# Last feed-forward chunk in three token groups, and its down product tile by tile, in a two-layer streaming encoder

## The chip, the core and the metric

One core of a Trainium2 chip runs the whole program in one launch. The metric is device time in microseconds (us) of an execution; below it is the median of three runs. A profile of one more execution gives the span from its first to its last instruction and every instruction with its times. The engines are TensorE (PE; its weight loads are PEld), VectorE (DVE), ScalarE (ACT), GpSimd (POOL) and SyncE (SP), which only issues DMAs here.

## The reference

Two trunk layers of an encoder act on 1024 tokens of one new stream and 16 new tokens of each of 8 running streams, 1152 rows of width 1024. A layer is a mixer (attention and a linear recurrence, concatenated, one output projection) and a convolutional feed-forward part, each followed by a post-norm residual:

```python
def conv_ffn(x, conv_prev, w_up, conv_w, conv_b, w_down):      # D_FF = 2816, CONV_W = 3
    u = x @ w_up                                               # (T, 2 * D_FF)
    ue = jnp.concatenate([conv_prev, u], 1)                    # two rows before the stream's first
    c = conv_b
    for j in range(CONV_W):
        c = c + ue[:, j:j + T] * conv_w[j]                     # depthwise, causal
    a, b = jnp.split(c, 2, axis=-1)
    y = (jax.nn.silu(a) * b) @ w_down
    return y, ue[:, -(CONV_W - 1):]
...
x = layer_norm(DN_ALPHA * x + m, ...)
f, c = conv_ffn(x, ...)
x = layer_norm(DN_ALPHA * x + f, ...)
```

All of it is float32. The change touches only the end of `conv_ffn` and the layer norm behind it.

## The kernel before, in words

The change is in `phase_trunk`, which runs once per layer: mixer output projection, first norm, feed-forward, second norm. Each engine has its own instruction list written out by hand; the lists are ordered among themselves only by semaphores (`wait_ge`, `then_inc`). SyncE's list holds the DMAs.

**Numbers as pairs.** A float32 operand of a product is held as two rounded parts, hi and lo; ScalarE writes hi (a copy), GpSimd or VectorE writes lo (a subtraction), and `mm3` (lines 124 to 126) does three matmuls for one product.

**Feed-forward.** The 2816 channels go in NJ = 22 chunks of 128, for each of the halves a (`ab` = 0) and b (`ab` = 1). For chunk j, `up(j)` projects both halves for three groups of 384 tokens (`up_part(ab, q)`, 24 matmuls, result in PSUM bank q). ScalarE evicts each (`take`, into `u`), applies the convolution's centre tap for the whole half (`centre_tap`, into `cv`), VectorE adds the two other taps (`conv`), ScalarE does SiLU on half a, VectorE multiplies (`gate`), ScalarE writes hi of the result (`silu_and_hi`, into `gh`) and GpSimd lo (`split_gate`). GpSimd also puts the running streams' old rows into `u` (`halos`), keeps the last rows (`keep_state`) and splits the weights (`split_up`, `split_down`). `down(j)` is then the product with the chunk's rows of `w_down`, 9 token tiles by 2 halves of 512 columns, each added into `XM` (the residual, `x_or_mix` in the trace) by VectorE (`add`).

**Chunk order.** In the steady loop the order on TensorE is `up(j+1)`, `down(j)`. The last chunks differ: `up(LAST-1)` and `up(LAST)` run first (LAST = 21), and the down products of chunks 19, 20 and 21 are then accumulated in PSUM tile by tile. `tail_two(t)` does the 12 matmuls of chunks 19 and 20 for token tile t, `tail_end(t)` the 6 of chunk 21, in a pair of banks (`tail_pair`): tiles 0 to 3 take pairs 0 to 3, tile t from 4 on takes pair (t-4) mod 3. `tail_two` of tiles 0 to 3 comes first, then TensorE waits for the whole of chunk 21's gate (`gs`) and its down weights (`dsp`), and then runs `tail_end(0)` to `tail_end(3)` and, for each later tile, `tail_two(t)`, `tail_end(t)`.

**Second norm.** VectorE runs, per tile, `tail_add(t)` (PSUM into `XM`), `fnorm.stats(t)`, and `fnorm.rstd(t)`; between them ScalarE does a square root (`root`), and after them `normalise(t)`. GpSimd multiplies by the gain (`scale`), then GpSimd or, for the last tile (and for odd tiles in layer 1), VectorE adds the bias (`add_bias`). SyncE stores the tile.

**Transposes in layer 0 (`more`).** The next layer wants its input transposed, as a pair. TensorE transposes a finished tile with 8 matmuls into two banks (`f_t(t)`, banks `f_banks(t)`: 6 and 7, or 4 and 5 for t = 4, 6, 8), ScalarE writes hi (`f_hi(t)`, tile `xT_hi`), VectorE lo (`f_lo(t)`, tile `xT_lo`). In the order before, `f_t(t-3)` follows `tail_end(t)`, ScalarE's `f_hi(t-3)` precedes `root(t)`, and VectorE's `f_lo(t-3)` stands between `stats(t)` and `rstd(t)`, each for t from 3 to 8; the last three tiles follow behind. `f_t` waits for the bias of its tile and for the `f_lo` that frees its banks:

```python
            def f_t(t):
                pe.wait_ge(fnorm.xr, t + 1)
                if t == 0:
                    pe.wait_ge(ad, 1 + ADDED + 4)
                elif t == 4:
                    pe.wait_ge(ad, 1 + ADDED + 7)
                else:
                    pe.wait_ge(fxlo, t if t < 4 else t - 1)
```

`ad` counts adds: `1 + ADDED + n` is reached when n tiles of the tail are added.

Of the kernel before, what the change touches and what calls it, by code (L numbers as in the profile page):

```python
# [1738 lines left out]
def phase_trunk(c, block, layer, m, L):  # L1739
# [32 lines left out]

    ghz = m.at(tag + "gh_last", 16384, [P, TOK], R)
    glz = m.at(tag + "gl_last", 20992, [P, TOK], R)
    dhz = m.at(tag + "dhi_last", 25600, [P, D], R)
    dlz = m.at(tag + "dlo_last", 83200, [P, D], R)
    fg = m.at(tag + "ffn_gain", 87296, [P, D])
# [56 lines left out]
    if True:  # L1834
        @block.sync
        def _(sp):
# [263 lines left out]
        def _(act):  # L2100
# [104 lines left out]
            for t in range(NT):  # L2205
                if more and t >= 3:
                    f_hi(t - 3)
                fnorm.root(act, t)
                fnorm.normalise(act, t)
            if more:  # L2210
                for t in range(NT - 3, NT):
                    f_hi(t)

        @block.vector
        def _(dve):
# [90 lines left out]
            for t in range(NT):  # L2306
                tail_add(t)
                dve.wait_ge(ad, 1 + ADDED + t + 1)
                fnorm.stats(dve, flink, t)
# [4 lines left out]
                fnorm.rstd(dve, flink, t)
            if more:
                f_lo(NT - 3)
                f_lo(NT - 2)
            else:
# [235 lines left out]
```

## Time and profile before

| | |
|---|---|
| median of 3 runs | 3154.3 us |
| lowest, highest | 3151.47, 3155.53 us |
| the profiled execution | 3158.42 us |
| its span | 3156.7 us |
| its mean granted TensorE clock | 0.970 of full |
| PE busy | 2973.2 us, 94% |
| DVE busy | 1649.6 us, 52% |
| ACT busy | 1032.7 us, 33% |
| POOL busy | 839.4 us, 27% |

Busy time is that of instructions at work; waits, semaphores and the issue of DMAs are not in it. The span is shorter than the execution's time, which has a start and an end around it. Lines with L and a number are lines of the kernel printed above; a row of the timeline has the start in us from the span's start, the duration, the engine, the line, the operation, what it writes and reads, and in brackets how long the engine had been idle before it and what released it.

### The profile page before, as it was taken

To read this page: it belongs to the slowest core of one execution; us is meant where nothing else is said; L and a number is where in the kernel's file an instruction comes from. 1 tells how busy PE (TensorE), PEld (TensorE's weight loads), DVE (VectorE), ACT (ScalarE), POOL (GpSimd) and SP (SyncE) were. 2 spreads that over 40 slices of the span, in tenths; PEclk is the share of its full clock that TensorE was granted. 3 is DMA by queue.
4 is the path that set the end of the run, shared out by engine and by line. 5 is a ranking of instruction groups with operands and counts; after the bars stand their busy time and mean duration, and the time that the engine had idled before them with its cause. 6 is when DMAs were issued, how large, how long until landed. Compare 5 with 4: busy or idle time off the path is not lost. (4 is left out here: it accounts for less than half of the span.)

```text
span 3156.7 us, 42325 instructions
## 1 busy us (share of the span) xinstructions
PE 2973.2 (94%) x15759; PEld 2609.2 (83%) x15759; DVE 1649.6 (52%) x2579; ACT 1032.7 (33%) x2001; POOL 839.4 (27%) x700
## 2 busy tenths in 40 slices
PE   8899789998999999999997898998999999999996
PEld 6455457886889999999996897997889999999995
DVE  3466224566545555555555443345445555555555
ACT  4334212233342232223223353334342222322323
POOL 1245211111132233322336000011132223232325
PEclk9999899998999999999998997998999999999998
DMA  2100331113111111111111111113111111111111
GB/s 104 39 8 8 119 135 43 38 38 112 41 59 40 40 40 46 41 47 40 41 40 65 49 35 39 28 42 115 41 52 47 40 40 40 47 41 45 40 40 73
DMA packets 71879, 160.47 MB, mean 51 GB/s; under 512 B 19194, under 2 KB 33675, under 8 KB 70708
## 3 DMA queue, kind: packets, MB, share of 16 engines
q1 hardware_dynamic: 70612, 150.51, 15.1%
q0 software_dynamic: 1152, 8.39, 0.7%
q8 instruction: 76, 1.25, 0.2%
q14 instruction: 39, 0.32, 0.0%
HBM read 144.42 MB, written 15.11 MB: 51 GB/s over the span
## 5 line engine op out<-in xcount | busy, mean ns | idle before, releaser
L124 PE MATMUL psum<-xT_hi,tk_whi 128*128 128x384 f32 x2112 | 711.4, 337 | 2.9 <-POOL tk_wlo L1892 1.6
L125 PE MATMUL psum<-xT_lo,tk_whi 128*128 128x384 f32 x2112 | 710.2, 336 | 0.0
L126 PE MATMUL psum<-xT_hi,tk_wlo 128*128 128x384 f32 x2112 | 710.1, 336 | 0.0
L2272 DVE TENSOR_TENSOR x_or_mix<-x_or_mix,psum 128x512 f32<-128x512 f32 x684 | 466.0, 688 | 220.9 <-PE psum L126 220.6
L124 PEld LDWEIGHTS psum<-xT_hi,tk_whi 128*128 128x128 f32 x2112 | 397.6, 188 | 5.7 <-ACT tk_u L2128 4.2
L125 PEld LDWEIGHTS psum<-xT_lo,tk_whi 128*128 128x128 f32 x2112 | 397.6, 188 | 1.6
L126 PEld LDWEIGHTS psum<-xT_hi,tk_wlo 128*128 128x128 f32 x2112 | 397.4, 188 | 0.0
L2257 DVE SCALAR_TENSOR_TENSOR tk_c<-tk_u,tk_cw,tk_c 128x1168 f32<-128x1168 f32 x88 | 126.1, 1433 | 457.7 <-ACT tk_c L2136 457.7
L124 PE MATMUL psum<-tk_dhi,tk_gh 128*128 128x512 f32 x756 | 295.4, 391 | 4.6 <-DVE x_or_mix L2277 2.9
L126 PE MATMUL psum<-tk_dhi,tk_gl 128*128 128x512 f32 x756 | 295.2, 390 | 0.0
L125 PE MATMUL psum<-tk_dlo,tk_gh 128*128 128x512 f32 x756 | 295.2, 390 | 0.0
L1892 POOL TENSOR_TENSOR tk_wlo<-tk_wraw,tk_whi 128x1024 fp32r<-128x1024 f32 x88 | 230.9, 2624 | 184.8 <-ACT tk_whi L2115 184.8
L1916 POOL TENSOR_TENSOR tk_gl<-tk_g,tk_gh 128x1152 fp32r<-128x1152 f32 x42 | 112.4, 2677 | 511.8 <-ACT tk_gh L2143 511.8
L2259 DVE SCALAR_TENSOR_TENSOR tk_c<-tk_u,tk_cw,tk_c 128x1168 f32<-128x1168 f32 x88 | 219.3, 2492 | 11.1 <-DVE tk_c L2257 5.4
L2143 ACT ACTIVATE tk_gh<-tk_g 128x1152 fp32r<-128x1152 f32 x42 | 49.0, 1166 | 517.1 <-DVE tk_g L2267 517.1
L124 PEld LDWEIGHTS psum<-tk_dhi,tk_gh 128*128 128x128 f32 x756 | 142.2, 188 | 34.1 <-DVE x_or_mix L2277 3.3
L126 PEld LDWEIGHTS psum<-tk_dhi,tk_gl 128*128 128x128 f32 x756 | 142.0, 188 | 29.9
L125 PEld LDWEIGHTS psum<-tk_dlo,tk_gh 128*128 128x128 f32 x756 | 142.2, 188 | 28.6
L571 POOL TENSOR_SCALAR mla_p<-mla_p,mla_ri 128x128 f32<-128x128 f32 (+7 forms) x64 | 110.1, 1723 | 207.0 <-DVE mla_ri L600 207.0
L2125 ACT ACTIVATE tk_u<-psum 128x384 f32<-128x384 f32 x176 | 85.4, 487 | 235.7 <-PE psum L126 235.7
L2127 ACT ACTIVATE tk_u<-psum 128x256 f32<-128x256 f32 x88 | 33.8, 384 | 312.9 <-PE psum L126 312.9
L124 PE MATMUL psum<-tk_mix_w,xT_hi 128*128 128x512 f32 x288 | 121.1, 420 | 14.7 <-POOL tk_mix_w L813 8.1
(367 smaller groups left out, 5280.7 us busy)
## 6 DMA issues: line engine op xcount, KB each, us to landing
tk_wraw<-in_w_up SPq DMA_DIRECT2D x88, 512.0 KB, 3.6
tk_draw<-in_w_down SPq DMA_DIRECT2D x44, 512.0 KB, 3.6
x_or_mix<-in_c_ckvT SPq DMA_DIRECT2D x8, 1024.0 KB, 5.7
s_ckv<-in_c_ckv POOLq DMA_DIRECT2D x8, 1024.0 KB, 5.0
retw_raw<-in_w_ret SPq DMA_DIRECT2D x32, 256.0 KB, 3.8
tk_mix_wraw<-in_w_out SPq DMA_DIRECT2D x16, 512.0 KB, 3.6
glaw_raw<-in_w_gla SPq DMA_DIRECT2D x32, 192.0 KB, 3.5
x_or_mix<-in_xT SPq DMA_DIRECT2D x9, 512.0 KB, 9.9
```

The costliest lines, as they stand in the source:

```text
L124: nc.tensor.matmul(out, a[0], b[0], start=first, stop=False)
L125: nc.tensor.matmul(out, a[0], b[1], start=False, stop=False)
L126: return nc.tensor.matmul(out, a[1], b[0], start=False, stop=last)
L571: nc.gpsimd.tensor_scalar(p, p, ri[:, u % 4:u % 4 + 1], None, ALU.mult).then_inc(scl, 1)
L1892: nc.gpsimd.tensor_tensor(wlo[:, ab].rearrange("p k n -> p (k n)"), wraw[:, ab, :], whi[:, ab].rearrange("p k n -> p (k n)").bitcast(F), A ...
L1916: nc.gpsimd.tensor_tensor(lo, gf[:], hi.bitcast(F), ALU.subtract).then_inc(gs, 1)
L2125: last = nc.scalar.activation(u[:, ab, 2 + q * GRP:2 + (q + 1) * GRP], PS[:, q, 0:GRP], ACT.Copy)
L2127: nc.scalar.activation(u[:, ab, 2 + 2 * GRP:US], PS[:, 2, 0:SEQ - 2 * GRP], ACT.Copy)
L2143: nc.scalar.activation(hi, gf[:], ACT.Copy).then_inc(ghd, 1)
L2257: nc.vector.scalar_tensor_tensor(cv[:, ab, 2:], u[:, ab, 1:UW - 1], cw[:, ab, col4(j, 1)], cv[:, ab, 2:], ALU.mult, ALU.add).then_inc(cch, 1)
L2259: nc.vector.scalar_tensor_tensor(cv[:, ab, 2:], u[:, ab, 0:UW - 2], cw[:, ab, col4(j, 0)], cv[:, ab, 2:], ALU.mult, ALU.add).then_inc(cvd, 1)
L2272: nc.vector.tensor_tensor(x, x, PS[:, down_bank(n), :], ALU.add).then_inc(ad, 1)
```

## The change

What it does:

- `up(LAST)` runs its six parts in the order (a,0), (a,1), (b,0), (b,1), (a,2), (b,2) instead of a's three and then b's three. The banks stay the group's number, and the waits for evictions follow the new order.
- The centre tap, convolution, SiLU, gate, hi and lo of chunk 21 are done in three groups of 384 tokens (the third has the running streams' rows). `ghz` and `glz`, one tile each, become three tiles each (`gz`), and the places of the last down weights and of the norm's gain move.
- TensorE does `tail_two(0)`, `tail_two(1)`, then `tail_end(0)`, `tail_end(1)`, and from tile 2 on `tail_two(t)`, `tail_end(t)`; tiles 0, 3 and 6 wait for their group of the gate. The bank pair of tile t is t mod 3 throughout, so pairs 0 to 2 are used and banks 6 and 7 are free.
- In layer 0 a table `F_AFTER` says after which tile's `tail_end` which `f_t` comes; `f_hi` and `f_lo` follow one tile later. `f_t(0)` waits for no add any more.
- The norm's gain is loaded when the last up part is done, the bias when the third group's convolution is done.

```diff
-    tail_pair = lambda t: t if t < 4 else (t - 4) % 3
-    f_banks = lambda t: 4 if t >= 4 and t % 2 == 0 else 6
+    tail_pair = lambda t: t % 3
+    f_banks = lambda t: 0 if t in (4, 6, 8) else 6
+    F_AFTER = {4: (0,), 5: (1,), 6: (2,), 7: (3,), 8: (4, 5)}
+    CONVS = 2 * NJ + 4
+    GROUPS = ((0, GRP, GRP), (GRP, 2 * GRP, GRP), (2 * GRP, SEQ, UW - 2 - 2 * GRP))
...
@@ sync
-            sp.wait_ge(us, 2 * NJ)
+            sp.wait_ge(um, 6 * NJ)
             sp.dma_start(fg[:], A["ln_ffn_g"][layer].partition_broadcast(P)).then_inc(fgl, 16)
-            sp.wait_ge(cvd, 2 * NJ)
+            sp.wait_ge(cvd, CONVS)
...
@@ gpsimd
+            def split_gate_group(g):
+                pool.wait_ge(ghd, LAST + g + 1)
+                nc.gpsimd.tensor_tensor(gz[1][g][:], gf[:, g * GRP:(g + 1) * GRP], gz[0][g][:].bitcast(F), ALU.subtract).then_inc(gs, 1)
...
             halos(LAST)
+            split_gate_group(0)
+            split_down(LAST, None)
+            split_gate_group(1)
             for ab in range(2):
-                keep_state(LAST, ab, 6 * LAST + 3 * ab + 3)
-            split_down(LAST, None)
-            split_gate(LAST, None)
+                keep_state(LAST, ab, 6 * LAST + 5 + ab)
+            split_gate_group(2)
...
@@ tensor
             def f_t(t):
                 pe.wait_ge(fnorm.xr, t + 1)
-                if t == 0:
-                    pe.wait_ge(ad, 1 + ADDED + 4)
-                elif t == 4:
+                if t == 4:
                     pe.wait_ge(ad, 1 + ADDED + 7)
-                else:
+                elif t:
                     pe.wait_ge(fxlo, t if t < 4 else t - 1)
...
             def tail_two(t):
-                pe.wait_ge(ad, 1 + ADDED + (0 if t < 4 else TAIL_AFTER[t - 4] + 1))
+                pe.wait_ge(ad, 1 + ADDED + max(t - 2, 0))
...
             def tail_end(t):
-                tail_down(t, (ghz, glz), (dhz, dlz), False, True).then_inc(dm, 1)
+                if t % 3 == 0:
+                    pe.wait_ge(gs, LAST + t // 3 + 1)
+                for half in range(2):
...
-            up(LAST)
+            for p, (ab, q) in enumerate(ORDER0):
+                if q == 0:
+                    pe.wait_ge(us, 2 * LAST + ab + 1)
+                pe.wait_ge(ur, 6 * LAST + (-2, -1, 1, 2, 0, 5)[p])
+                up_part(ab, q)
             pe.wait_ge(gs, LAST - 1)
             pe.wait_ge(dsp, LAST - 1)
             pe.wait_ge(ur, 6 * NJ)
-            for t in range(4):
-                tail_two(t)
-            pe.wait_ge(gs, LAST + 1)
+            tail_two(0)
+            tail_two(1)
             pe.wait_ge(dsp, LAST + 1)
             for t in range(NT):
-                if t >= 4:
+                if t >= 2:
                     tail_two(t)
                 tail_end(t)
-                if more and t >= 3:
-                    f_t(t - 3)
+                if more:
+                    for f in F_AFTER.get(t, ()):
+                        f_t(f)
...
@@ scalar
             def hi_down(j, par):
                 act.wait_ge(ld, 16 * j + 16)
+                if par is None:
+                    act.wait_ge(um, 6 * LAST + 5)
...
-            for ab in range(2):
-                act.wait_ge(cvd, 2 * LAST + ab - 1)
-                act.wait_ge(sk, 2 * LAST + ab - 1)
-                for q in range(3):
-                    take(ab, q, 6 * LAST + 3 * ab + q)
-                centre_tap(LAST, ab, 6 * LAST + 3 * ab + 3)
-            hi_down(LAST, None)
-            silu_and_hi(LAST, None)
+            for p, (ab, q) in enumerate(ORDER0):
+                if q == 0:
+                    act.wait_ge(cvd, 2 * LAST + ab - 1)
+                    act.wait_ge(sk, 2 * LAST + ab - 1)
+                take(ab, q, 6 * LAST + p)
+                if p == 2:
+                    centre_group(0)
+                if p == 3:
+                    centre_group(1)
+                    silu_group(0)
+                    hi_group(0)
+                if p == 4:
+                    hi_down(LAST, None)
+                    silu_group(1)
+                    hi_group(1)
+            centre_group(2)
+            silu_group(2)
+            hi_group(2)
...
             for t in range(NT):
-                if more and t >= 3:
-                    f_hi(t - 3)
+                if more:
+                    for f in F_AFTER.get(t - 1, ()):
+                        f_hi(f)
                 fnorm.root(act, t)
                 fnorm.normalise(act, t)
             if more:
-                for t in range(NT - 3, NT):
+                for t in range(4, NT):
                     f_hi(t)
...
@@ vector
+            def gate_group(g):
+                a, b, _ = GROUPS[g]
+                dve.wait_ge(si, LAST + g + 1)
+                dve.wait_ge(cvd, 2 * LAST + 2 * g + 2)
...
-            conv(LAST, 0)
-            conv(LAST, 1)
-            gate(LAST)
+            for g in range(3):
+                conv_group(g)
+                gate_group(g)
...
                 fnorm.stats(dve, flink, t)
                 if t >= 2 and by_dve(t - 2):
                     fnorm.add_bias(dve, nc.vector, t - 2, fodd)
-                if more and t >= 3:
-                    f_lo(t - 3)
+                if more:
+                    for f in F_AFTER.get(t - 1, ()):
+                        f_lo(f)
                 fnorm.rstd(dve, flink, t)
             if more:
-                f_lo(NT - 3)
-                f_lo(NT - 2)
+                for t in range(4, NT - 1):
+                    f_lo(t)
```

`centre_group(g)`, `silu_group(g)` and `hi_group(g)` on ScalarE and `conv_group(g)` on VectorE are the whole-chunk operations on a group's columns; `conv_group` has two taps for each half, as `conv` has.

## Rows read from the trace of the kernel before

**Rows 1.** The page, part 1: busy time, share of the span and instructions of each engine.

```profile
PE 2973.2 (94%) x15759; PEld 2609.2 (83%) x15759; DVE 1649.6 (52%) x2579; ACT 1032.7 (33%) x2001; POOL 839.4 (27%) x700
```

**Rows 2.** The timeline of VectorE, end of layer 0.

```profile
1684.57 1.22 DVE L2277 TENSOR_TENSOR x_or_mix<-x_or_mix,psum 128x1024 f32<-128x1024 f32 x1 [5.70 <-PE psum L126]
...
1689.68 1.22 DVE L2277 TENSOR_TENSOR x_or_mix<-x_or_mix,psum 128x1024 f32<-128x1024 f32 x1 [0.15 <-DVE tk_f_negmean L1720]
...
1693.44 1.22 DVE L2277 TENSOR_TENSOR x_or_mix<-x_or_mix,psum 128x1024 f32<-128x1024 f32 x1
...
1701.61 1.23 DVE L2303 TENSOR_TENSOR xT_lo<-psum,xT_hi 128x1024 fp32r<-128x1024 f32 x1 [1.62 <-ACT xT_hi L2203]
...
1705.47 1.22 DVE L2277 TENSOR_TENSOR x_or_mix<-x_or_mix,psum 128x1024 f32<-128x1024 f32 x1 [2.31 <-PE psum L126]
...
1708.40 1.23 DVE L2303 TENSOR_TENSOR xT_lo<-psum,xT_hi 128x1024 fp32r<-128x1024 f32 x1
...
1725.49 1.22 DVE L2277 TENSOR_TENSOR x_or_mix<-x_or_mix,psum 128x1024 f32<-128x1024 f32 x1 [0.53 <-PE psum L126]
...
1739.76 1.23 DVE L2303 TENSOR_TENSOR xT_lo<-psum,xT_hi 128x1024 fp32r<-128x1024 f32 x1 [3.12 <-ACT xT_hi L2203]
```

**Rows 3.** Busy time by stretches, layer 0's end; PEclk is the granted clock's share of full.

```profile
core 0: us, PE busy (x) PEld busy (x) DVE busy (x) ACT busy (x) POOL busy (x), PEclk, DMA share, GB/s
1688.60:1698.50 9.90, 0.01 (x1) 0.00 (x0) 7.83 (x16) 4.78 (x7) 7.35 (x4) 0.66 0.13 53
1698.50:1701.50 3.00, 2.93 (x11) 2.77 (x12) 1.45 (x3) 0.95 (x2) 3.00 (x2) 0.50 0.07 26
...
1727.40:1731.20 3.80, 0.01 (x1) 0.00 (x0) 2.35 (x6) 1.43 (x2) 3.69 (x2) 0.76 0.26 105
```

**Rows 4.** The timeline of TensorE, end of layer 0.

```profile
1671.25 0.47 PE L124 MATMUL psum<-tk_dhi,tk_gh 128*128 128x512 f32 x1 [0.85 <-ACT tk_u L2128]
...
1682.88 0.50 PE L124 MATMUL psum<-tk_dhi_last,tk_gh_last 128*128 128x512 f32 x1 [0.49 <-POOL tk_gl_last L1916]
...
1698.57 1.94 PE L2017 MATMUL psum<-ident,x_or_mix 128*128 128x128 f32 x8 [9.96 <-DVE x_or_mix L2277]
...
1705.27 1.03 PE L2017 MATMUL psum<-ident,x_or_mix 128*128 128x128 f32 x8
...
1710.28 1.03 PE L2017 MATMUL psum<-ident,x_or_mix 128*128 128x128 f32 x8
...
1731.22 1.97 PE L2017 MATMUL psum<-ident,x_or_mix 128*128 128x128 f32 x8 [3.81 <-POOL x_or_mix L1736]
1736.70 1.97 PE L2017 MATMUL psum<-ident,x_or_mix 128*128 128x128 f32 x8 [3.51 <-DVE x_or_mix L1736]
```

**Rows 5.** The timeline of ScalarE, last up chunk and tail of layer 0.

```profile
1655.28 0.85 ACT L2125 ACTIVATE tk_u<-psum 128x384 f32<-128x384 f32 x2
...
1666.27 0.49 ACT L2125 ACTIVATE tk_u<-psum 128x384 f32<-128x384 f32 x1 [3.58 <-PE psum L126]
1670.44 0.38 ACT L2127 ACTIVATE tk_u<-psum 128x256 f32<-128x256 f32 x1 [3.67 <-PE psum L126]
...
1730.07 1.24 ACT L1726 ACTIVATE x_or_mix<-x_or_mix,tk_f_negmean,tk_f_mv 128x1024 f32<-128x1024 f32 x1 [1.40 <-DVEq L1721]
```

**Rows 6.** The timeline of VectorE, last chunk of layer 0: second taps.

```profile
1661.51 1.44 DVE L2259 SCALAR_TENSOR_TENSOR tk_c<-tk_u,tk_cw,tk_c 128x1168 f32<-128x1168 f32 x1
...
1673.89 3.46 DVE L2259 SCALAR_TENSOR_TENSOR tk_c<-tk_u,tk_cw,tk_c 128x1168 f32<-128x1168 f32 x1
```

**Rows 7.** The timeline of GpSimd, weight splits around the last chunk.

```profile
1648.72 2.71 POOL L1892 TENSOR_TENSOR tk_wlo<-tk_wraw,tk_whi 128x1024 fp32r<-128x1024 f32 x1 [2.21 <-ACT tk_whi L2115]
...
1673.41 2.70 POOL L1904 TENSOR_TENSOR tk_dlo_last<-tk_draw,tk_dhi_last 128x1024 fp32r<-128x1024 f32 x1 [2.05 <-ACT tk_dhi_last L2120]
```

**Rows 8.** The timeline of VectorE, end of layer 1.

```profile
3107.97 1.22 DVE L2277 TENSOR_TENSOR x_or_mix<-x_or_mix,psum 128x1024 f32<-128x1024 f32 x1 [5.69 <-PE psum L126]
...
3151.28 1.23 DVE L1736 TENSOR_TENSOR x_or_mix<-x_or_mix,tk_ffn_bias 128x1024 f32<-128x1024 f32 x1 [2.23 <-POOL x_or_mix L1731]
```

More of the change, by code:

```diff
@@ L1771, in phase_trunk @@
     cw = m.at(tag + "cw", 95488, [P, 2, NJ * 4])
[L1773 to L1777, printed above, removed]
+    gz = [[m.at(f"{tag}g{part}_last{g}", at, [P, GRP], R) for g, at in enumerate(places)]
+          for part, places in (("h", (83200, 84736, 20480)), ("l", (86272, 87808, 22016)))]
+    dhz = m.at(tag + "dhi_last", 16384, [P, D], R)
+    dlz = m.at(tag + "dlo_last", 24576, [P, D], R)
+    fg = m.at(tag + "ffn_gain", 28672, [P, D])
     fb = m.at(tag + "ffn_bias", 32768, [P, D])
@@ L1903, in split_down @@
                 lo, hi = (dlz[:], dhz[:]) if par is None else (dlo[:, par, :], dhi[:, par, :])
+                if par is None:
+                    pool.wait_ge(um, 6 * LAST + 5)
                 nc.gpsimd.tensor_tensor(lo, draw[:], hi.bitcast(F), ALU.subtract).then_inc(dsp, 1)
@@ L1914, in split_gate @@
                 pool.wait_ge(ghd, j + 1)
-                lo, hi = (glz[:], ghz[:]) if par is None else (gl[:, par, :], gh[:, par, :])
-                nc.gpsimd.tensor_tensor(lo, gf[:], hi.bitcast(F), ALU.subtract).then_inc(gs, 1)
+                nc.gpsimd.tensor_tensor(gl[:, par, :], gf[:], gh[:, par, :].bitcast(F), ALU.subtract).then_inc(gs, 1)
+            def split_gate_group(g):
+                pool.wait_ge(ghd, LAST + g + 1)
+                nc.gpsimd.tensor_tensor(gz[1][g][:], gf[:, g * GRP:(g + 1) * GRP], gz[0][g][:].bitcast(F), ALU.subtract).then_inc(gs, 1)
             def step(j, par):
@@ L2033, in tail_end @@
             def tail_end(t):
-                tail_down(t, (ghz, glz), (dhz, dlz), False, True).then_inc(dm, 1)
+                if t % 3 == 0:
+                    pe.wait_ge(gs, LAST + t // 3 + 1)
+                for half in range(2):
+                    cs = slice(half * 512, half * 512 + 512)
+                    xs = slice(t % 3 * P, t % 3 * P + P)
+                    end = mm3(nc, PS[:, 2 * tail_pair(t) + half, :], (gz[0][t // 3][:, xs], gz[1][t // 3][:, xs]), (dhz[:, cs], dlz[:, cs]), False, True)
+                end.then_inc(dm, 1)
             mix_t(0)
@@ L2118, in hi_down @@
                 act.wait_ge(ld, 16 * j + 16)
+                if par is None:
+                    act.wait_ge(um, 6 * LAST + 5)
                 hi = dhz[:] if par is None else dhi[:, par, :]
@@ L2141, in silu_and_hi, with centre_group, silu_group, hi_group @@
                 act.wait_ge(gr, j + 1)
-                hi = ghz[:] if par is None else gh[:, par, :]
-                nc.scalar.activation(hi, gf[:], ACT.Copy).then_inc(ghd, 1)
+                nc.scalar.activation(gh[:, par, :], gf[:], ACT.Copy).then_inc(ghd, 1)
+            def centre_group(g):
+                a, _, n = GROUPS[g]
+                if g == 0:
+                    act.wait_ge(gr, LAST)
+                for ab in range(2):
+                    act.wait_ge(ur, 6 * LAST + ((1, 3), (2, 4), (5, 6))[g][ab])
+                    if g == 2:
+                        act.wait_ge(hl, 2 * LAST + ab + 1)
+                    nc.scalar.activation(cv[:, ab, 2 + a:2 + a + n], u[:, ab, 2 + a:2 + a + n], ACT.Identity, bias=cw[:, ab, col4(LAST, 3)],
+                                         scale=cw[:, ab, col4(LAST, 2)]).then_inc(c0, 1)
+            def silu_group(g):
+                a, _, n = GROUPS[g]
+                act.wait_ge(cvd, 2 * LAST + 2 * g + 1)
+                nc.scalar.activation(cv[:, 0, 2 + a:2 + a + n], cv[:, 0, 2 + a:2 + a + n], ACT.Silu).then_inc(si, 1)
+            def hi_group(g):
+                act.wait_ge(gr, LAST + g + 1)
+                nc.scalar.activation(gz[0][g][:], gf[:, g * GRP:(g + 1) * GRP], ACT.Copy).then_inc(ghd, 1)
             def step(j, par):
@@ L2259, in conv, with conv_group @@
                 nc.vector.scalar_tensor_tensor(cv[:, ab, 2:], u[:, ab, 0:UW - 2], cw[:, ab, col4(j, 0)], cv[:, ab, 2:], ALU.mult, ALU.add).then_inc(cvd, 1)
+            def conv_group(g):
+                a, _, n = GROUPS[g]
+                for ab in range(2):
+                    i = 2 * LAST + 2 * g + ab
+                    out = cv[:, ab, 2 + a:2 + a + n]
+                    dve.wait_ge(c0, i + 1)
+                    nc.vector.scalar_tensor_tensor(out, u[:, ab, 1 + a:1 + a + n], cw[:, ab, col4(LAST, 1)], out, ALU.mult, ALU.add).then_inc(cch, 1)
+                    dve.wait_ge(cch, i + 1)
+                    nc.vector.scalar_tensor_tensor(out, u[:, ab, a:a + n], cw[:, ab, col4(LAST, 0)], out, ALU.mult, ALU.add).then_inc(cvd, 1)
+            def gate_group(g):
+                a, b, _ = GROUPS[g]
+                dve.wait_ge(si, LAST + g + 1)
+                dve.wait_ge(cvd, 2 * LAST + 2 * g + 2)
+                if g == 0:
+                    dve.wait_ge(gs, LAST)
+                last = nc.vector.tensor_tensor(gf[:, a:b], cv[:, 0, 2 + a:2 + b], cv[:, 1, 2 + a:2 + b], ALU.mult)
+                if g == 2:
+                    new_a, new_b = (cv[:, ab, US:].rearrange("p (b t) -> p b t", b=NB)[:, :, 2:] for ab in range(2))
+                    last = nc.vector.tensor_tensor(gf[:, SEQ:].rearrange("p (b t) -> p b t", b=NB), new_a, new_b, ALU.mult)
+                last.then_inc(gr, 1)
             def gate(j):
```

1 line of the change is left out of this document (removed).

## The prediction

> **What bounds the kernel now.** I read the page's busy shares first, then the end of each layer engine by engine, then the granted clock of short stretches there. TensorE is busy 94% of the span [rows 1], and the change takes no matmul away: what it can move are stretches where TensorE waits, or where it works for an engine that waits. There are two such ends, one in each layer, and they begin with the same pattern. TensorE finishes the last up chunk, has stood 0.85 us when ScalarE's last eviction releases it, then does four tiles' share of the two older chunks and waits 0.49 us for GpSimd's `gl_last` (1671.25 to 1682.88; 48 matmuls, so 0.23 us each) [rows 4]. The first `tail_add` starts at 1684.57 in layer 0 and at 3107.97 in layer 1 [rows 2, 8].
>
> From there the layers differ. In layer 1 VectorE is the bound: nine tiles of add, statistics and, for odd tiles, bias, from 3107.97 to 3152.5, 44.5 us [rows 8]. In layer 0 each tile is also transposed for the next layer. TensorE has stood for 9.96 us when the add of tile 3 lets it begin a round per tile: 8 transposes (`f_t`), 18 matmuls. Adds then follow every 5.01 us (1705.47 to 1725.49, four rounds), which is TensorE's pace (5.01 from 1705.27 to 1710.28, transposes and matmuls) [rows 2, 4]. There VectorE's `f_lo(n)` is a round ahead of TensorE's want: it runs in tile n+3's iteration, and `f_t(n+1)` follows tile n+4. From the last add 15.5 us of chain are left, to the end of f_lo(8) at 1740.99 [rows 2].
>
> **The change, part by part.** Times are in layer 0's frame; up to the first add layer 1 is the same.
>
> *Order of the up parts.* A part is 24 matmuls, 4.17 us (two evictions apart, 1666.27 to 1670.44) [rows 5]; the chunk's six run from 1645.4 to 1670.4. ScalarE, which waits for the chunk before, can evict the first part only at 1655.28 [rows 5]. Now the third part goes to the third bank and this costs nothing; in the new order it is (1,0) and writes the first bank, so it starts at 1655.8 instead of 1653.8: 2.0 us. The last two, (0,2) and (1,2), share the third bank, and the second waits for the eviction of the first: 0.55 and two handovers, 0.7 us. The up chunk ends 2.7 us later, at 1673.1. The weights of half b are wanted a part earlier, at 1653.8; their split ends at 1651.4 [rows 7], so nothing.
>
> *Three groups.* ScalarE's centre taps, SiLU and copies and VectorE's taps and gates become three times as many at a third of the length. The trace has no such size; a whole tap takes 1.44 [rows 6], so a third takes between 0.48 (all by length) and 0.96 (half of it fixed); I take 0.6. Groups 0 and 1 lie beside the up parts, group 2 beside the first two tiles' 24 matmuls (5.5 us, against some 4.5 us of taps, SiLU and gate), so their sum costs nothing; with 0.96 the last gate would be done about when the first tile is, and cost some 0.5. What can cost is queueing on ScalarE: its last eviction, for which TensorE waits, now stands behind the copy of group 1, and that behind gate 1. GpSimd splits `dlo_last` (2.70) [rows 7] from about 1670.0; gate 1 comes due at 1670.6. A VectorE tap that fell beside that split took 3.46, one beside an idle GpSimd 1.44 [rows 6]; so the gate ends near 1673.4, the copy 0.5 later, and the eviction at 1674.6 instead of 1673.7, a cost of 0.9 (ends: 0 if the gate isn't held, 1.5 if GpSimd's group-0 split delays it too).
> The Trainium skill (SBUF — State Buffer, "SBUF: two separate sides") says that GpSimd and a VectorE instruction with two SBUF inputs take a shared port pair as an exclusive lock for the whole instruction. The gate reads two SBUF tensors, so by that page it is held as well and the cost is 0.9; were the taps alone held, it would be 0 and the sum 1.8 less over both layers. The tap's row agrees; for a gate no row shows it.
>
> *Tail by tile.* TensorE starts tile 0 at 1674.8 (3.5 later) and needs two tiles' 24 matmuls (5.5) instead of four tiles' 48 and the 0.49 of waiting: the first product of the last chunk starts at 1680.3 instead of 1682.88. The first add moves from 1684.57 to 1682.0: **−2.6 us in each layer**. In layer 1 TensorE then delivers a tile every 4.1 us from 2.8 us behind the first product on, and VectorE takes 5.11 for the first [rows 2] and 44.5 for all nine, so TensorE is never late and the 2.6 is kept to the end. The gain load moves from before the tail to its start, the bias load little; GpSimd wants both 6 us after the first add. No DMA is on the path; the stores of x1 and y follow their tiles. A bank is freed by the add three tiles back, over 2 us before it is wanted.
>
> *Transposes of layer 0.* This is where the time goes. `F_AFTER` puts `f_t(n)` after tile n+4, and ScalarE's `f_hi(n)` and VectorE's `f_lo(n)` into iteration n+5. `f_t(n+1)` still waits for `f_lo(n)`; both use banks 6 and 7. But `f_lo(n)` now stands behind the add of tile n+5, and `f_t(n+1)` comes right behind that very tile's matmuls. Nothing overlaps any more. A round is f_t and 18 matmuls up to the add 5.20 (1705.27 to 1710.47 by pace), add to f_lo 2.93 (1705.47 to 1708.40), f_lo 1.23: **9.36 us** instead of 5.01 [rows 2, 4]. Behind the waiting `f_t` the whole next tile is queued, and VectorE's next add waits for that.
> By the clock of a steady round: adds 0 to 5 go at VectorE's pace, 1682.0 + 5.11 + 4 × 3.76 = 1702.15 [rows 2]. f_lo(0) ends at 1706.3; TensorE, done with tile 5 at 1680.3 + 2.8 + 4 × 4.1 + 1.0 = 1700.5, has stood for 5.8. Adds 6, 7 and 8 come at 1711.5, 1720.9, 1730.2. Now the last is at 1725.49. **+4.8 us.**
> After the last add five transposed tiles instead of three are unfinished. f_lo(3) ends 4.1 after the add, normalise(8) and f_hi(4) 2.7 later, f_lo(4) and (5) 2.4, f_t(7) 2.0, f_hi(7) 1.1, f_lo(7) 1.2, bias(8) 1.2, f_t(8) 2.0, f_hi(8) and f_lo(8) 2.3 [rows 2, 4, 5, 8]: 19.0 against 15.5, and 0.3 if f_t(6) is slow too. **+3.8 us.**
> *Clock.* Over the 9.9 us stand the granted clock averaged 0.66, and it was 0.50 (1.2 of 2.4 GHz) for the first 3.0 us of work behind it; a 3.80 us stretch without matmuls brought it down too (0.76 on average), and the 8 transposes then took 1.97 instead of 1.03 [rows 3, 4]. The new stands are 5.8, 4.2 and 4.2 us, so I expect the clock down in each. The one restart with tile matmuls here took 6.70 us (1698.57 to 1705.27) where 5.01 is the steady pace [rows 4]: 1.7. Bounds per stand are 0 (the clock stays) and 5.0 (a whole round at half). I take 2.2: near that row, a little over, since one row may be a lucky one. **+6.6 us.**
>
> Sum: layer 0 4.8 + 3.8 + 6.6 = 15.2 (its earlier first add is in the 1682.0), layer 1 −2.6, together **+12.6 us**. The profiled execution took 3158.42 us with a span of 3156.7; 12.6 more is 3171.0. The runs' median, 3154.3, lies 4.1 below it, and the sum is the same there: 3166.9.
>
> **The rivals.**
> A: the same serial rounds, but the clock stays up. 4.8 + 3.5 − 2.6 = +5.7, 3160.0. For it: after the short stands, 0.85 and 0.49, matmuls go on at the fast pace [rows 4]. Against: the 3.80 us row, shorter than every new stand.
> B, the other side: `f_lo(n)` is done before TensorE wants it, and rounds go at 5.01. Adds 6 to 8 follow 1702.15 to 1717.2, 8.3 earlier; unfinished tiles +3.8; layer 1 −2.6: −7.1, 3147.2. It decides at `f_t(1)`: TensorE would have to be done with tile 5 5.8 us later than I work out (at 0.23 a matmul there is no such room), or VectorE at f_lo(0) that much earlier, which its order, behind add 5, excludes.
> C: the start gains nothing. If gate 1, ScalarE's queue and GpSimd's splits cost 2.6 more than I think, the first adds stay where they are: +17.8, 3172.1. For it: three or four handovers per group that no row prices. Against: of all that only the last eviction is on the path.
>
> **How the numbers follow.** Forecast 0.72, its own range 3161 (clock 1.7 a stand, first adds 1.5 earlier) to 3171 (3.5 a stand); A 0.08, B 0.08, C 0.07, the rest 0.05. The range for 8 in 10 is 3159 to 3172. About 0.2%, 6.3 us, is what a measurement of this kernel can tell from no change; slower begins at 3160.6. That is the forecast and C, 0.79, and a bit of the rest; A and what is left, 0.12, lie within; faster is B, 0.08.
>
> **What would show it.** The third and sixth up part of the last chunk start 2.0 and 0.7 late, released by ScalarE's evictions; first adds are 2.6 earlier in both layers; in layer 0 adds 5 to 8 lie more than 9 us apart, with TensorE stands of about 6, 4 and 4 us before `f_t`, released by VectorE's `f_lo`, and a granted clock below 1 behind them; 19 us pass from the last add to the last f_lo. Wrong would be adds 5 us apart (B), 9.4 apart at clock 1.0 (A), or first adds at the old place (C).

## The result and the profile after

The changed kernel takes 3167.62 us (median of 7 runs, 3163.46 to 3169.8), the kernel before in the same comparison 3155.53 (7 runs, 3150.66 to 3161.21): ratio 1.0030, 95% interval 1.0018 to 1.0042. It is slower, by 12.1 us between the medians; the interval excludes no change.

Busy times hardly move (page, part 1); TensorE's count of instructions is the same as in [rows 1]:

```profile
PE 2976.5 (94%) x15759; PEld 2611.9 (83%) x15759; DVE 1655.9 (52%) x2599; ACT 1036.0 (33%) x2017; POOL 841.9 (27%) x704
```
Runs drift against each other by a few us before either tail. So I count from the start of ScalarE's pair of first evictions of the last up chunk (in [rows 5] 1655.28; 3078.69 in layer 1 before), and call the time from there "the tail's clock" (it is a way to count time, and has nothing to do with TensorE's granted clock). The changed kernel, ScalarE, layer 0 (timeline: start, duration, engine, line, what it does, idle time before and what ended it):

```profile
1657.14 0.85 ACT L2144 ACTIVATE tk_u<-psum 128x384 f32<-128x384 f32 x2
...
1674.95 0.52 ACT L2181 ACTIVATE tk_gh_last<-tk_g 128x384 fp32r<-128x384 f32 x1 [2.51 <-DVE tk_g L2326]
1675.60 0.38 ACT L2146 ACTIVATE tk_u<-psum 128x256 f32<-128x256 f32 x1
```
and in layer 1:

```profile
3090.80 0.86 ACT L2144 ACTIVATE tk_u<-psum 128x384 f32<-128x384 f32 x2
```
| from the first evictions, us | before | after |
|---|---|---|
| layer 0: first add | 29.29 | 26.38 |
| layer 0: adds of tiles 5, 6, 7, 8 | 55.19, 60.20, 65.21, 70.21 | 46.55, 57.43, 69.59, 80.74 |
| layer 0: end of the last f_lo | 85.71 | 100.31 |
| layer 1: first add | 29.28 | 26.37 |
| layer 1: end of the last bias | 73.82 | 70.91 |

Layer 0 loses 14.6 us, layer 1 gains 2.9: +11.7 in sum. The profiled span grew by 9.2 only (3165.9 against 3156.7); the other 2.5 lie in stretches that the change doesn't touch (last section).

VectorE in layer 0 of the changed kernel: two gates, the adds of tiles 0, 5, 6, 7 and 8, and f_lo(0), (1) and (8). They answer to [rows 2].

```profile
1668.50 0.56 DVE L2326 TENSOR_TENSOR tk_g<-tk_c 128x384 f32<-128x384 f32 x1 [2.63 <-ACT tk_c L2177]
...
1672.47 2.44 DVE L2326 TENSOR_TENSOR tk_g<-tk_c 128x384 f32<-128x384 f32 x1 [0.30 <-ACT tk_c L2177]
...
1683.52 1.22 DVE L2348 TENSOR_TENSOR x_or_mix<-x_or_mix,psum 128x1024 f32<-128x1024 f32 x1 [3.47 <-PE psum L126]
...
1703.69 1.22 DVE L2348 TENSOR_TENSOR x_or_mix<-x_or_mix,psum 128x1024 f32<-128x1024 f32 x1
...
1706.62 1.23 DVE L2374 TENSOR_TENSOR xT_lo<-psum,xT_hi 128x1024 fp32r<-128x1024 f32 x1
...
1714.57 1.22 DVE L2348 TENSOR_TENSOR x_or_mix<-x_or_mix,psum 128x1024 f32<-128x1024 f32 x1 [6.40 <-PE psum L126]
...
1717.50 1.23 DVE L2374 TENSOR_TENSOR xT_lo<-psum,xT_hi 128x1024 fp32r<-128x1024 f32 x1
...
1726.73 1.22 DVE L2348 TENSOR_TENSOR x_or_mix<-x_or_mix,psum 128x1024 f32<-128x1024 f32 x1 [7.68 <-PE psum L126]
...
1737.88 1.22 DVE L2348 TENSOR_TENSOR x_or_mix<-x_or_mix,psum 128x1024 f32<-128x1024 f32 x1 [6.68 <-PE psum L126]
...
1756.22 1.23 DVE L2374 TENSOR_TENSOR xT_lo<-psum,xT_hi 128x1024 fp32r<-128x1024 f32 x1 [3.12 <-ACT xT_hi L2251]
```
The second gate took 2.44 us where the first took 0.56. GpSimd was splitting the last down weights beside it, from 1672.10 to 1674.50:

```profile
1672.10 2.40 POOL L1908 TENSOR_TENSOR tk_dlo_last<-tk_draw,tk_dhi_last 128x1024 fp32r<-128x1024 f32 x1 [1.00 <-ACT tk_dhi_last L2139]
```
f_lo(0) starts 2.93 us after the add of tile 5 as before, but the next add comes 7.95 us behind it: rounds of 10.88, 12.16 and 11.15 us, where they were 5.01. TensorE, to set beside [rows 4]:

```profile
1657.75 0.42 PE L124 MATMUL psum<-xT_hi,tk_whi 128*128 128x384 f32 x1 [2.14 <-ACT tk_u L2144]
...
1671.13 0.44 PE L124 MATMUL psum<-xT_hi,tk_whi 128*128 128x384 f32 x1 [0.64 <-ACT tk_u L2147]
...
1676.41 0.47 PE L124 MATMUL psum<-tk_dhi,tk_gh 128*128 128x512 f32 x1 [0.85 <-ACT tk_u L2147]
...
1707.99 1.94 PE L2024 MATMUL psum<-ident,x_or_mix 128*128 128x128 f32 x8 [5.91 <-DVE xT_lo L2374]
...
1718.88 1.94 PE L2024 MATMUL psum<-ident,x_or_mix 128*128 128x128 f32 x8 [4.34 <-POOL x_or_mix L1736]
...
1731.03 1.72 PE L2024 MATMUL psum<-ident,x_or_mix 128*128 128x128 f32 x8 [4.34 <-DVE xT_lo L2374]
...
1742.18 1.94 PE L2024 MATMUL psum<-ident,x_or_mix 128*128 128x128 f32 x8 [3.47 <-DVE xT_lo L2374]
```
The first two are the up parts that wait for an eviction, the third is tile 0 of the tail, at 19.27 in the tail's clock where it was 15.97 before. The `f_t` rows are f_t(1), (2), (3) and (5), each behind a stand of 3.5 to 5.9 us. The row of 1718.88 names GpSimd's bias as releaser; f_lo(1) ended at 1718.73 and that bias, of tile 5, which f_t(2) doesn't wait for, at 1718.81, so I take it that the view chose between two near events and that f_lo(1) released TensorE. The granted clock over the three rounds, then in the first 3 us of work after each stand (columns as in [rows 3]):

```profile
1703.70:1737.90 34.20, 21.22 (x81) 17.44 (x81) 12.68 (x22) 9.76 (x11) 24.40 (x11) 0.80 0.19 77
1708.00:1711.00 3.00, 3.00 (x12) 2.76 (x13) 0.17 (x1) 2.27 (x2) 3.00 (x2) 0.53 0.31 124
1718.80:1721.80 3.00, 2.92 (x11) 2.76 (x12) 0.21 (x1) 2.19 (x2) 1.35 (x2) 0.50 0.43 175
1731.00:1734.00 3.00, 2.97 (x12) 2.71 (x13) 0.20 (x1) 2.27 (x2) 1.39 (x1) 0.55 0.00 0
```
Layer 1, first add and last bias, beside [rows 8]; everything between follows at VectorE's pace, as before:

```profile
3117.17 1.22 DVE L2348 TENSOR_TENSOR x_or_mix<-x_or_mix,psum 128x1024 f32<-128x1024 f32 x1 [3.47 <-PE psum L126]
...
3160.48 1.23 DVE L1736 TENSOR_TENSOR x_or_mix<-x_or_mix,tk_ffn_bias 128x1024 f32<-128x1024 f32 x1 [2.23 <-POOL x_or_mix L1731]
```

### The profile page after: what moved, and what is told of

Its sections match the earlier page's. It is cut to its first block and busy times, and to the rows that moved or that the text cites. A ratio compares the mean times of both kernels' runs of the same rounds, so it can differ in the third digit from the quotient of the medians.

```text
span 3165.9 us, 42374 instructions
## 1 busy us (share of the span) xinstructions
PE 2976.5 (94%) x15759; PEld 2611.9 (83%) x15759; DVE 1655.9 (52%) x2599; ACT 1036.0 (33%) x2017; POOL 841.9 (27%) x704
## 5 line engine op out<-in xcount | busy, mean ns | idle before, releaser
L2306 DVE SCALAR_TENSOR_TENSOR tk_c<-tk_u,tk_cw,tk_c 128x1168 f32<-128x1168 f32 x84 | 120.3, 1433 | 428.1 <-ACT tk_c L2155 428.1
L2308 DVE SCALAR_TENSOR_TENSOR tk_c<-tk_u,tk_cw,tk_c 128x1168 f32<-128x1168 f32 x84 | 209.6, 2495 | 11.0 <-DVE tk_c L2306 5.4
```

What stands on the lines that cost most here:

```text
L2306: nc.vector.scalar_tensor_tensor(cv[:, ab, 2:], u[:, ab, 1:UW - 1], cw[:, ab, col4(j, 1)], cv[:, ab, 2:], ALU.mult, ALU.add).then_inc(cch, 1)
```

## The experiments

Theory: `f_t(n+1)` waits for an `f_lo(n)` that VectorE does only after the add of the tile which TensorE finishes right before `f_t(n+1)`; the two engines take turns, and behind each stand TensorE's granted clock is down for a while. Rivals: banks and GpSimd's queue; the stands alone without the clock; the groups and the new part order. Times "in the tail's clock" come from each run's own profile. All ratios are against the kernel before, run beside them on the same chip (there were two chips: the kernel before had 3158.18 us beside the runs "one tile earlier", "stands filled", "six banks" and "layer 1 alone", and 3159.49 beside the other four).

**f_hi and f_lo one tile earlier.** TensorE's list is untouched.

```diff
-                if more:
-                    for f in F_AFTER.get(t - 1, ()):
-                        f_lo(f)
+                if more and t >= 4:
+                    f_lo(t - 4)
```

(f_hi likewise, and f_lo(4) leaves the list behind the loop.)

> Against the changed kernel: in layer 0, f_hi(t-4) and f_lo(t-4) run in iteration t on ScalarE and VectorE, not one iteration later; TensorE's order is the same. Serial-round theory: VectorE's f_lo(n) is done before TensorE comes to f_t(n+1), rounds return to about 5.0 us, no TensorE stand over 1 us between tiles 4 and 8, clock 1.0 there; last add some 18 us earlier than in the changed kernel (about 1720 in its frame, where it was 1737.9), chain behind it about 18 us; whole kernel about 19 to 20 us faster than the changed one and 7 to 8 us faster than the one before (3147 to 3148 where before is 3155.5). Rival, that the loss sits in what is queued on GpSimd or in the bank pairs shared by three tiles: rounds stay over 8 us and the time stays within 5 us of the changed kernel's.

Measured: 3149.13 us, ratio 0.9954 (0.9937 to 0.9972). VectorE's adds of tiles 5 to 8 and the last f_lo, then f_t(1) on TensorE:

```profile
1703.86 1.22 DVE L2347 TENSOR_TENSOR x_or_mix<-x_or_mix,psum 128x1024 f32<-128x1024 f32 x1
...
1710.27 1.22 DVE L2347 TENSOR_TENSOR x_or_mix<-x_or_mix,psum 128x1024 f32<-128x1024 f32 x1 [1.93 <-PE psum L126]
...
1715.27 1.22 DVE L2347 TENSOR_TENSOR x_or_mix<-x_or_mix,psum 128x1024 f32<-128x1024 f32 x1 [0.53 <-PE psum L126]
...
1720.28 1.22 DVE L2347 TENSOR_TENSOR x_or_mix<-x_or_mix,psum 128x1024 f32<-128x1024 f32 x1 [0.53 <-PE psum L126]
...
1736.91 1.23 DVE L2373 TENSOR_TENSOR xT_lo<-psum,xT_hi 128x1024 fp32r<-128x1024 f32 x1 [3.12 <-ACT xT_hi L2251]
```
```profile
1703.54 1.94 PE L2024 MATMUL psum<-ident,x_or_mix 128*128 128x128 f32 x8 [2.14 <-DVE xT_lo L2373]
```
The last two rounds take 5.0 us. The first takes 6.41, because VectorE is behind TensorE until tile 5: f_t(1) still stood 2.14 us and ran at the low clock (1.94 us), against the expectation's "no TensorE stand over 1 us". Layer 0 ends at 81.67 in the tail's clock, 18.6 earlier than in the changed kernel and 4.0 earlier than before. The median is 9.0 below that of the kernel before, where 7 to 8 was expected. So the loss hangs on the place of f_hi and f_lo in the lists; the two were moved together and not tried apart. GpSimd and the banks were as in the changed kernel, so that rival falls.

**Same order, but f_t waits two back.** If the wait is the cause and not the place by itself, a second pair of banks for the transposes must cure it too.

```diff
-    tail_pair = lambda t: t % 3
-    f_banks = lambda t: 0 if t in (4, 6, 8) else 6
+    tail_pair = lambda t: t % 2
+    f_banks = lambda t: 4 if t % 2 else 6
...
-                elif t:
-                    pe.wait_ge(fxlo, t if t < 4 else t - 1)
+                if t > 1:
+                    pe.wait_ge(fxlo, t - 1)
...
-                pe.wait_ge(ad, 1 + ADDED + max(t - 2, 0))
+                pe.wait_ge(ad, 1 + ADDED + max(t - 1, 0))
```

> Against the changed kernel: same order on every engine, f_lo(n) still in iteration n+5. Only banks and waits differ: the tail's tiles alternate between two bank pairs (0-1, 2-3) instead of three, the transposes between two pairs (6-7, 4-5), so f_t(n+1) waits for f_lo(n-1) and not for f_lo(n). Theory (the loss is the wait for the f_lo just behind the add of the same tile, one pair of banks deep): f_t(1) to f_t(3) start without a stand over 1 us, rounds are 5.0 to 5.5 us, first add as in the changed kernel, layer 0 ends some 17 to 19 us earlier than in it; whole about 3149, like the run with f_lo one tile earlier. Rival (the late place of f_lo by itself is the loss, whatever the banks): rounds stay over 8 us. Cost of one pair less for the tail: tile t waits for the add of t-2, at most 1.5 us at tile 2, hidden in layer 1.

Measured: 3142.61 us, ratio 0.9951 (0.9935 to 0.9967). Adds 5 to 8, and the stretch with its granted clock, which is 1.00:

```profile
1701.73 1.22 DVE L2346 TENSOR_TENSOR x_or_mix<-x_or_mix,psum 128x1024 f32<-128x1024 f32 x1
...
1706.46 1.22 DVE L2346 TENSOR_TENSOR x_or_mix<-x_or_mix,psum 128x1024 f32<-128x1024 f32 x1 [0.25 <-PE psum L126]
...
1711.46 1.22 DVE L2346 TENSOR_TENSOR x_or_mix<-x_or_mix,psum 128x1024 f32<-128x1024 f32 x1 [0.53 <-PE psum L126]
...
1716.47 1.22 DVE L2346 TENSOR_TENSOR x_or_mix<-x_or_mix,psum 128x1024 f32<-128x1024 f32 x1 [0.53 <-PE psum L126]
```
```profile
1701.70:1716.50 14.80, 14.80 (x79) 12.39 (x78) 12.70 (x22) 7.79 (x10) 14.56 (x7) 1.00 0.26 106
```
Rounds of 4.7 to 5.0, layer 0's end 19.1 earlier than in the changed kernel. `f_lo` is exactly as late in the order as there, so with a second pair of banks its place costs nothing; the late place and the single pair together do. One pair less for the adds cost nothing measurable (first adds and layer 1's end within 0.03). The median is 6 us below the 3149 expected, and the tails don't show where that comes from (last section).

**The stands filled.** 20, 14 and 14 extra matmuls behind tiles 5, 6, 7, into banks that the next tile overwrites.

```diff
+                if more and t in (5, 6, 7):
+                    pe.wait_ge(ad, 1 + ADDED + t - 1)
+                    for n in range(20 if t == 5 else 14):
+                        nc.tensor.matmul(PS[:, 2 * tail_pair(t + 1), :], gh[:, 1, 0:P], dhi[:, 1, 0:512], start=True, stop=True)
```

> Against the changed kernel: TensorE does 20, 14 and 14 extra 128x512 matmuls (into the banks of the next tile, which overwrites them) behind tiles 5, 6 and 7, in the stretch where it stands and waits for VectorE's f_lo. They add 4.5, 3.2 and 3.2 us of work inside stands of 5.9, 4.3 and 4.4 us. Clock term of my prediction: the granted clock stays at 1.0 through the three rounds, each round goes from 11.4 us to the 9.36 us worked out for full clock, so 6 us less in all, about 3161.5. Rival: the stand itself, not the clock, is all of the loss, and the rounds are long for another reason: then rounds stay at 11 us or grow by what the extra matmuls take.

Measured: 3157.6 us, ratio 0.9994 (0.9981 to 1.0007). Adds 5 to 8 on VectorE, f_t(1) and f_t(2) on TensorE, and the clock over the three rounds:

```profile
1703.23 1.22 DVE L2352 TENSOR_TENSOR x_or_mix<-x_or_mix,psum 128x1024 f32<-128x1024 f32 x1
...
1712.76 1.22 DVE L2352 TENSOR_TENSOR x_or_mix<-x_or_mix,psum 128x1024 f32<-128x1024 f32 x1 [5.05 <-PE psum L126]
...
1722.30 1.22 DVE L2352 TENSOR_TENSOR x_or_mix<-x_or_mix,psum 128x1024 f32<-128x1024 f32 x1 [5.06 <-PE psum L126]
...
1731.81 1.22 DVE L2352 TENSOR_TENSOR x_or_mix<-x_or_mix,psum 128x1024 f32<-128x1024 f32 x1 [5.03 <-PE psum L126]
```
```profile
1707.54 1.06 PE L2024 MATMUL psum<-ident,x_or_mix 128*128 128x128 f32 x8 [1.38 <-DVE xT_lo L2378]
...
1717.07 1.07 PE L2024 MATMUL psum<-ident,x_or_mix 128*128 128x128 f32 x8 [1.17 <-DVE xT_lo L2378]
```
```profile
1703.20:1731.80 28.60, 24.88 (x122) 20.07 (x121) 12.68 (x21) 9.48 (x11) 23.50 (x11) 1.00 0.23 92
```
With 48 more matmuls the kernel is faster than the changed one. The waits are as long, only filled; rounds take 9.53 us at clock 1.00 where they averaged 11.40 at 0.80. From the add of tile 5 to that of tile 8 pass 28.58 us instead of 34.19: the clock was worth 5.6 us. Layer 0 ends 5.6 earlier (94.67 in the tail's clock) and layer 1 as in the changed kernel. The median is 10.0 lower, more than that, and the rest does not lie in the tails.

**Six banks for the last up chunk.** `up_part` and `take` use bank q + 3·ab, and half b waits for the adds of chunk 18 instead of evictions.

```diff
-                pe.wait_ge(ur, 6 * LAST + (-2, -1, 1, 2, 0, 5)[p])
-                up_part(ab, q)
+                if ab == 0:
+                    pe.wait_ge(ur, 6 * LAST + q - 2)
+                elif q == 0:
+                    pe.wait_ge(ad, 1 + ADDED)
+                up_part(ab, q, q + 3 * ab)
```

> Against the changed kernel: the last up chunk's three parts of half b go to PSUM banks 3, 4 and 5 instead of 0, 1 and 2, so no part waits for an eviction of its own chunk. The two TensorE stands of 2.14 and 0.64 us in the last up chunk go, in both layers. Theory: the chunk ends 3.0 us earlier, but ScalarE's last eviction then stands behind the copy of group 1, behind gate 1, which VectorE can't run beside GpSimd's weight split; so the first add comes 2.1 us earlier in each layer, not 3.0, and the whole is 4.2 us faster than the changed kernel. Rival, all handovers of the groups are hidden: 3.0 each, 6.0 in all. Rival, the first add is bound elsewhere (weights' split, group 0): under 1 us each.

Measured: 3163.13 us, ratio 1.0011 (0.9998 to 1.0024). Copy of group 1 and last eviction on ScalarE, then the first add:

```profile
1673.52 0.52 ACT L2186 ACTIVATE tk_gh_last<-tk_g 128x384 fp32r<-128x384 f32 x1 [2.51 <-DVE tk_g L2331]
1673.95 0.37 ACT L2151 ACTIVATE tk_u<-psum 128x256 f32<-128x256 f32 x1
```
```profile
1681.84 1.22 DVE L2353 TENSOR_TENSOR x_or_mix<-x_or_mix,psum 128x1024 f32<-128x1024 f32 x1 [3.41 <-PE psum L126]
```
First adds come 2.65 us earlier in both layers, between the theory's 2.1 and the rival's 3.0. Both had a term wrong: the up chunk ends 3.3 earlier and not 3.0, and the last eviction is held behind the copy of group 1 for 0.7 us and not 0.9. Layer 1 keeps the gain to its end (68.27). Layer 0 ends only 1.3 earlier (99.00), for its three rounds took 12.02, 11.14 and 12.36 us, 35.5 instead of 34.2, with TensorE's stands as long as before (5.91, 4.34, 4.34).

**And the SiLU and copy of group 1 behind that eviction.** `silu_group(1)` and `hi_group(1)` move from p = 4 to p = 5.

> Against the changed kernel: six banks for the last up chunk (as in the run with six banks) and ScalarE's SiLU and copy of group 1 behind its last eviction instead of ahead. With six banks alone the first adds came 2.65 us earlier in both layers, and the last eviction still began 0.9 us after its part was done, behind group 1's copy. Theory: that 0.9 goes, first adds 3.5 to 3.6 us earlier than in the changed kernel in both layers. Rival: group 1 and 2 then come late on VectorE and its first add waits for gate 2 instead: no gain over six banks alone, or a loss.

Measured: 3159.48 us, ratio 0.9999 (0.9990 to 1.0008). The first add:

```profile
1686.32 1.22 DVE L2354 TENSOR_TENSOR x_or_mix<-x_or_mix,psum 128x1024 f32<-128x1024 f32 x1 [1.68 <-PE psum L126]
```
It is at 23.1 in the tail's clock, 3.3 earlier than in the changed kernel, 0.65 more than with the banks alone, in both layers. That is less than the 3.5 to 3.6 expected, since there was 0.7 to gain and not 0.9. VectorE had been idle for 1.68 us when TensorE released it, so gate 2 isn't in the way. Layer 0 ends 3.0 earlier (rounds of 12.37, 11.15 and 10.94), layer 1 3.3.

**The change in layer 1 alone.** Layer 0 runs the trunk of the kernel before.

> Layer 0 runs the trunk of the kernel before, layer 1 that of the changed kernel, which is the half of the change without transposes. Theory: all of the loss is in layer 0's transposes, and layer 1's first add and end are 2.9 us earlier than before: 2.9 us faster than the kernel before (ratio 0.999), 15 us faster than the changed one. Rival, the groups and the new order cost in both layers: slower than before.

Measured: 3157.09 us against 3158.18, ratio 0.9996 (0.9984 to 1.0008), which can't tell 2.9 us from nothing. Its profile shows the gain: first add and last bias of layer 1 are at 26.36 and 70.92 in the tail's clock (which starts at 3073.70), against 29.28 and 73.82 before, and layer 0 ends at 85.69 as before (85.71):

```profile
3100.06 1.22 DVE L2348 TENSOR_TENSOR x_or_mix<-x_or_mix,psum 128x1024 f32<-128x1024 f32 x1 [3.40 <-PE psum L126]
...
3143.39 1.23 DVE L1736 TENSOR_TENSOR x_or_mix<-x_or_mix,tk_ffn_bias 128x1024 f32<-128x1024 f32 x1 [2.23 <-POOL x_or_mix L1731]
```

**All three repairs.** f_hi and f_lo a tile earlier, six banks, group 1 behind the eviction.

> Against the changed kernel: f_hi and f_lo one tile earlier, six banks, SiLU and copy of group 1 behind the last eviction. Theory, effects add up: layer 0 ends 18.6 + 3.5 us earlier than in the changed kernel, layer 1 3.5: 25.6 in all; against the kernel before 7.5 in layer 0 and 6.4 in layer 1, 13.9 in all, about 3142 to 3144 (ratio 0.9956). Rival: VectorE bounds layer 0's tail from the first add on, but GpSimd's gain and bias (4.9 us a tile from the first normalise) come to bound the transposes, and only 1 to 2 of the 3.5 arrive at layer 0's end.

Measured: 3140.70 us (before 3159.49 beside it), ratio 0.9934 (0.9913 to 0.9955). Layer 0 ends 22.4 earlier than in the changed kernel (18.6 + 3.3 would be 21.9), layer 1 3.3: the effects add up. It is faster than both kernels. f_t(1) stands 2.14 us here too, but its transposes take 1.06 us and not the 1.94 of the run "one tile earlier", so this time the clock stayed up:

```profile
1706.60 1.06 PE L2025 MATMUL psum<-ident,x_or_mix 128*128 128x128 f32 x8 [2.14 <-DVE xT_lo L2379]
```

**With the last tile's bias ahead of f_lo(6) and (7).**

> As the run with all three, and in layer 0 VectorE adds the last tile's bias right behind f_lo(5) instead of behind f_lo(7), so that f_t(8) follows f_t(7) directly. Theory: GpSimd's scale(8) is done 8.2 us after the last add, the bias then ends near 9.4, f_t(8) waits only for f_lo(6); the chain from last add to last f_lo is 14.5 to 15.5 us instead of 17.9: 2.5 to 3 us less than the run with all three, about 3140. Rival: f_lo(6) and (7), pushed back by the bias, become the chain's end and the gain is under 1 us.

Measured: 3138.35 us, ratio 0.9925 (0.9913 to 0.9938); not told apart from the version without it. VectorE's last add, bias and last f_lo:

```profile
1721.22 1.22 DVE L2353 TENSOR_TENSOR x_or_mix<-x_or_mix,psum 128x1024 f32<-128x1024 f32 x1 [0.53 <-PE psum L126]
...
1732.65 1.23 DVE L1736 TENSOR_TENSOR x_or_mix<-x_or_mix,tk_ffn_bias 128x1024 f32<-128x1024 f32 x1 [3.45 <-POOL x_or_mix L1731]
...
1738.19 1.22 DVE L2379 TENSOR_TENSOR xT_lo<-psum,xT_hi 128x1024 fp32r<-128x1024 f32 x1 [2.05 <-ACT xT_hi L2257]
```
From the last add to the end pass 18.2 us, against 18.9 in the run with all three: the rival's number (a gain under 1 us), but not its reason. The bias was free to run and stood 3.45 us for GpSimd's `scale(8)`, which I had put 8.2 us behind the add and which ended 11.4 us behind it, since GpSimd still had the gain and bias of older tiles to do.

## Why the prediction was right, step by step

- **Order of the up parts**, 2.0 and 0.7 us: the stands are there, 2.14 and 0.64 us, released by the evictions. The parts began 2.3 and 0.8 us behind the pace and each with a slower first matmul, so the chunk ended 3.3 us later and not 2.7 (its last matmul starts at 18.09 in the tail's clock where it was 14.78).
- **Gate 1 held by GpSimd's weight split**: held, 2.44 us where gate 0 took 0.56. The Trainium skill (SBUF — State Buffer, "SBUF: two separate sides") says that a VectorE instruction with two SBUF inputs is blocked for the whole of a GpSimd instruction that reads SBUF and started first. The trace agrees for the gate: its row ends at 1674.91, 0.41 us behind the split that was under way when it began. The price was wrong: 0.9 predicted, nothing paid. Group 1's copy ended at 1675.47, and the sixth part's last matmul started at 1675.23; the eviction followed that matmul by 0.37 us, as in the kernel before (0.38). The whole hold lay beside the late sixth part. With the stands gone it came out, 0.65.
- **First add**, −2.6: −2.9 in both layers. Two errors of opposite sign nearly cancel in it: tile 0 starts 3.3 later where 3.5 was predicted (its two terms, 2.7 and 0.9, give 3.6), because the order cost 0.6 more and the gate 0.9 less. That the number came so near is in part luck. Layer 1 keeps the gain whole to its end.
- **Serial rounds**, 9.36 at full clock: 9.53 with the stands filled. The last add was to come 4.8 late without the clock (the working's own 1730.2 gives 4.7) and comes 4.9 late there (75.12 against 70.21).
- **Clock**, 6.6 (2.2 a stand): 5.6 in sum, with the stands filled as the measure of full clock. This term rested on one row and its bounds were 0 and 15. Two stands of the same 4.34 us were followed by rounds of 12.16 and 11.15, 2.6 and 1.6 over 9.53; the same three stands cost 6.9 us in the profile with six banks and 5.9 with the late group 1 (35.5 and 34.5 us for the three rounds, less 28.6); and a stand of 2.14 us brought the clock down in one run and not in another. That the clock would fall was right. That it came to near 2.2 a stand was luck as much as judgement.
- **After the last add**, +3.8: 19.57 instead of 15.50, +4.1.
- **Sum**: +12.6 predicted, +11.7 in the tails, +12.1 between medians. Layer 0 was over by 0.6, layer 1's gain was 0.3 larger than predicted. The forecast of 3166.9 is 0.7 from the measured median, nearer than the terms warrant.
- Rival A (the clock stays up) fell with the granted clock of 0.80 over the rounds, B (f_lo done in time) with the stands before f_t, C (no gain at the start) with the first adds, which came 2.9 earlier.

## What to carry to other kernels

When two engines hand tiles back and forth, write for each wait where in the other engine's list its release stands and what that release itself waits for: a buffer one pair deep and a consumer placed one tile too late turned a pipeline of 5.0 us a tile into turns of 9.5 us, and of 11.4 with the low clock, with no engine busier than before. Moving the consumer a tile up, or a second buffer, gave back all of it. Where a stand of TensorE can't be avoided, its cost is the stand and the slow work behind it, here 5.6 us on three stands of 14.6 us together.

## What the runs showed of the hardware that I had not expected

From the end of layer 0's transposes to the first evictions of layer 1's last up chunk, no edit changes what has to be done, yet that stretch took from 1325.4 to 1337.7 us in the ten profiles. (Where the third up part waits, TensorE has done ten matmuls fewer, 1.7 us, when the stretch ends.) The two ends (columns as in [rows 3]), the kernel before and the one with filled stands:

```profile
1741.00:3078.70 1337.70, 1295.43 (x7131) 1206.78 (x7132) 686.83 (x1071) 451.60 (x904) 315.51 (x295) 0.97 0.15 46
```
```profile
1751.36:3076.80 1325.44, 1282.75 (x7121) 1195.87 (x7121) 688.15 (x1072) 451.69 (x903) 315.78 (x295) 0.98 0.15 46
```
VectorE, ScalarE and GpSimd are busy for the same time within 1.4 us. TensorE is not: 1295.4 against 1282.8, of which 1.7 are those ten matmuls. In these traces the granted clock was at 0.50 for 73.7 us of the one stretch and for 47.9 of the other, and the ten stretches go nearly in the order of that time (47.9 us low for 1325.4, 54.3 for 1328.8, 61.5 for 1332.4, 66.0 for 1333.4, 73.7 for 1337.7): 12.3 us more for 25.8 us more at half clock. So how the low-clock spells fall in a stage far from the change moves this kernel by some 10 us, as much as the change itself. Runs of one kernel show the same: of 30 executions of the kernel before, the fastest, 3150.76 us, had a mean granted clock of 0.974 and the slowest, 3168.78, one of 0.967, and over all 30 the correlation of time and clock is −0.95. The executions of one kernel spread over 6 to 22 us, so single medians (3157.6 for the filled stands) can't be read to a few us. What decides the length of a spell in those stages was not tried.

One thing stays open. Against the kernel before beside them, the medians fell further than the two tails account for: −16.9 us where the tails give −7.4 with f_t waiting two back, −18.8 and −14.0 with all three repairs, −0.6 and +6.1 with the stands filled. The profiles of these three had the shortest of the ten stretches above (1328.6, 1328.8 and 1325.4 us). Whether what TensorE does in layer 0's tail shortens the low-clock spells behind it, or whether that is chance, no run shows. The causes above rest on the tails, which don't depend on it.
